# One closing stage for the RWKV branch and the gated merge, with products of split weights, in a hybrid encoder layer

## The reference, cut to what matters

```
# RWKV branch, after the two scans; 8 heads of 64 channels
y = ys[0] + ys[1]
mu = mean(y, -1); var = mean(square(y - mu), -1)
y = ((y - mu) * rsqrt(var + GN_EPS)).reshape(B, S, 512) * gn_w + gn_b
bonus = sum(r_h * k * r_k, -1) * v_h
g = sigmoid(gd) @ gate_up
y_a = ((y + bonus) * g) @ w_o_rwkv
# MLA branch: o is the attention's output
y_b = o @ w_o_mla
x = x + gate1 * ((g_a * y_a + g_b * y_b) @ w_out)
```

## Time and profile before

| | us |
|---|---|
| median of 3 runs (3070.61 to 3104.45) | 3072.3 |
| the profiled execution, its own time | 3069.41 |
| its span, first to last instruction | 3067.5 |
| PE busy in the span (86%) | 2632.4 |
| DVE busy (45%) | 1381.7 |
| ACT busy (29%) | 903.7 |
| POOL busy (24%) | 722.6 |

### The profile page before, as it was taken

The page is one execution under the profiler, slowest core; times in us unless marked ns, Lnnn a source line. Parts: engine busy times, 40 slices in busy tenths (PEclk is TensorE's granted clock), DMA queues, the critical chain, the costliest instruction groups (busy, mean ns, idle before and its releaser), DMA issues. The chain is left out here.

```text
span 3067.5 us, 55849 instructions
## 1 busy us (share of the span) xinstructions
PE 2632.4 (86%) x23155; PEld 2022.6 (66%) x23155; DVE 1381.7 (45%) x1995; ACT 903.7 (29%) x1714; POOL 722.6 (24%) x563
## 2 busy tenths in 40 slices
PE   8699999999959999996988999657968952999990
PEld 2288887788849999996974555443437742788870
DVE  2544469866623555543544556442234340111116
ACT  2311133444413555443543444340012210111110
POOL 0122245444423444430332000220000003010003
PEclk9899999999966999996988999878989866999995
DMA  8312233443341232213338110332231113999977
GB/s 349 107 69 86 86 122 138 144 141 141 119 149 43 86 86 82 86 24 123 100 89 322 32 32 1 114 106 110 109 119 55 55 43 144 354 352 355 350 291 274
DMA packets 161343, 428.64 MB, mean 140 GB/s; under 512 B 38156, under 2 KB 85172, under 8 KB 147832
## 3 DMA queue, kind: packets, MB, share of 16 engines
q1 hardware_dynamic: 131432, 322.82, 30.6%
q0 software_dynamic: 15456, 53.50, 4.5%
q10 hardware_dynamic: 14256, 49.44, 4.0%
HBM read 302.94 MB, written 122.77 MB: 139 GB/s over the span
## 5 line engine op out<-in xcount | busy, mean ns | idle before, releaser
L99 PE MATMUL ps_in<-h_t_low,w_in_high 128*128 128x512 f32 x960 | 380.3, 396 | 20.8 <-DVE h_t_low L611 20.8
L100 PE MATMUL ps_in<-h_t_high,w_in_low 128*128 128x512 f32 x960 | 375.3, 391 | 0.0
L101 PE MATMUL ps_in<-h_t_high,w_in_high 128*128 128x512 f32 x960 | 374.9, 391 | 0.0
L2510 PE MATMUL ps_hidden<-xb_turned,w_tile 128*128 128x128 f32 x2176 | 248.1, 276 | 8.2 <-ACT xb_turned L2528 8.2
L2510 PEld LDWEIGHTS ps_hidden<-xb_turned,w_tile 128*128 128x128 f32 x2176 | 245.1, 192 | 12.0 <-ACT xb_turned L2528 12.0
L99 PEld LDWEIGHTS ps_in<-h_t_low,w_in_high 128*128 128x128 f32 x960 | 181.0, 189 | 63.3 <-issue 20.7
L101 PEld LDWEIGHTS ps_in<-h_t_high,w_in_high 128*128 128x128 f32 x960 | 181.1, 189 | 38.4
L1119 POOL TENSOR_TENSOR wkv_levels<-wkv_nt,level_mask 128x1024 f32<-128x1024 f32 x60 | 140.1, 2353 | 276.6 <-ACT wkv_nt L1068 276.6
L100 PEld LDWEIGHTS ps_in<-h_t_high,w_in_low 128*128 128x128 f32 x960 | 181.1, 189 | 36.1
L1880 PE MATMUL ps_scores<-att_k,att_q 96*128 96x512 f32 x320 | 168.0, 640 | 16.2 <-DMA att_q<-qk_t 16.2
L1968 DVE TENSOR_REDUCE att_neg_max<-ps_scores 128x1 f32<-128x1024 f32 (+1 forms) x96 | 100.5, 1047 | 115.7 <-PE ps_scores L1880 115.7
(11 more groups left out here) (344 smaller groups left out, 5197.8 us busy)
## 6 DMA issues: line engine op xcount, KB each, us to landing
w_tile<-in_w SPq DMA_DIRECT2D x34, 2048.0 KB, 9.3
w_tile<-in_w SPq DMA_DIRECT2D x34, 1024.0 KB
w_ada_tile<-in_w_ada SPq DMA_DIRECT2D x12, 2048.0 KB
wkv_in<-wkv_out SPq DMA_DIRECT2D x24, 1024.0 KB, 4.7
w_in_tile<-in_w_in SPq DMA_DIRECT2D x40, 512.0 KB, 5.7
yb<-yb_tile ACTq DMA_DIRECT2D x34, 512.0 KB, 9.4
yb<-att_zeros POOLq DMA_DIRECT2D x32, 512.0 KB, 35.4
p_t<-p_mixed ACTq DMA_DIRECT2D x24, 512.0 KB
```

The lines of the kernel that those rows point to most:

```text
L99: nc.tensor.matmul(out, w[0], x[1], start=start, stop=False)
L100: nc.tensor.matmul(out, w[1], x[0], start=False, stop=False)
L101: return nc.tensor.matmul(out, w[0], x[0], start=False, stop=stop)
L2510: mm = nc.tensor.matmul(ps_h[b][:, f], w13[:, b, k, P * f:P * f + P], xt[:, b, k], start=(k == 0), stop=(k == DF - 1))
```

## The change

`finish_and_merge` takes the place of `rwkv_finish` and `merge_branches`, in one block, unrolled.

- The merge has 48 units instead of 24: first 24 for MLA (output tile by output tile, three blocks of tokens each), then 24 for RWKV (block by block, eight output tiles each). A unit is 4 products of one branch, each by `split_product`, so 12 F32R products; DVE multiplies by one gate and, in the RWKV half, adds to `merged`.
- ACT makes the high parts of `om_t` (three blocks) and of each weight tile, DVE the low parts (`om_low`, `w_low`). MLA's 8 weight tiles are split once, RWKV's 8 tiles once for each block of tokens, 32 splits in all. The closing's result is written over `om_t`, whose blocks are split again (`oa_high`, `oa_low`).
- The closing's six tiles are dealt out between the units, a new tile every PITCH = 4 units, from unit 0 on: DVE has one or two steps of it behind each unit's gate (mean, centre, variance, normalise, bonus, affine, gated_out at 0, 1, 2, 3, 4, 6 and 7 units past the tile's start), PE has the bonus sums behind unit 4j+2 and the output gate and the turning behind unit 4j+5.
- Group norm is done by token: y stays with tokens on the partitions, mean and variance are DVE reductions over 64 channels (128x16 results of 128x1024), the root is ACT's Sqrt and DVE's reciprocal of 128x16, and y is turned once, after it is normed. The matrices of ones are scaled by r_k once, so that POOL's second multiplication goes. The tanh of the output gate is one instruction for all tokens.
- SP loads y for two tiles ahead, weights in 3 buffers, gates in 4 buffers of 128x512.

```diff
-def rwkv_finish(nc, dram, consts, oa_t):
...
-def merge_branches(nc, dram, consts, oa_t, om_t, merged):
...
+def finish_and_merge(nc, dram, consts, om_t, merged):
...
+        GB, RB, PITCH = 4, 3, 4
...
+        units = [(1, df, n) for df in range(DF) for n in range(NT)] + [(0, df, n) for n in range(NT) for df in range(DF)]
...
+        first_unit = lambda w: w * NT if w < DF else half + w - DF
...
+            def load_gate(u):
+                a, df, n = units[u]
+                if u >= GB:
+                    v = u - GB
+                    if v < half:
+                        sp.wait_ge(m["gated"], v + 1)
+                    else:
+                        sp.wait_ge(m["added"], v - half + 1)
+                sp.dma_start(gate[:, u % GB], dram["gates"][a * DF + df, :, cols(n)]).then_inc(g_in[u % GB], 16)
...
+            load_w(0)
+            load_y(0)
+            sp.dma_start(head_ones[:], dram["head_ones"][:, :]).then_inc(m["ones_in"], 16)
+            load_gate(0)
+            load_rk(0)
+            load_w(1)
+            sp.dma_start(sg[:], dram["p_t"][GD]).then_inc(m["gd_in"], 16)
+            sp.dma_start(up[:], dram["gate_up"][:, :]).then_inc(m["up_in"], 16)
+            for u in range(1, GB):
+                load_gate(u)
+            load_v(0)
+            load_y(1)
+            load_w(2)
+            loaded = RB
+            for u in range(len(units)):
+                if u + GB < len(units):
+                    load_gate(u + GB)
+                while loaded < len(tiles) and first_unit(loaded - RB) - 2 <= u:
+                    load_w(loaded)
+                    loaded += 1
+                for j in range(N):
+                    if u == PITCH * j + 3 and j + 1 < N:
+                        load_rk(j + 1)
+                    if u == PITCH * j + 5 and j + 1 < N:
+                        load_v(j + 1)
+                    if u == PITCH * j + 6 and j + 2 < N:
+                        load_y(j + 2)
...
+            sum_directions(0)
+            for j in range(N):
+                pool.wait_ge(m["rk_in"], 16 * j + 16)
+                nc.gpsimd.tensor_tensor(rkv[:, 0:4], rkv[:, 0:4], rkv[:, 4:8], ALU.mult).then_inc(m["rk"], 1)
+                if j + 1 < N:
+                    sum_directions(j + 1)
...
+                pe.wait_ge(m["w_lo"], w + 1)
+                if a == 1:
+                    pe.wait_ge(m["om_lo"], n + 1)
+                else:
+                    pe.wait_ge(m["oa_lo"], n + 1)
+                if u >= 2:
+                    pe.wait_ge(m["gated"], u - 1)
+                for f in range(RF):
+                    mm = split_product(nc, ps[:, u % 2], (w_hi[:, w % 2, f], w_lo[:, w % 2, f]), (src_hi[:, f, cols(n)], src_lo[:, f, cols(n)]),
+                                       start=(f == 0), stop=(f == RF - 1))
+                mm.then_inc(m["full"], 1)
...
+            for u in range(len(units)):
+                unit(u)
+                for j in range(N):
+                    if u == PITCH * j + 2:
+                        bonus_sums(j)
+                    if u == PITCH * j + 5:
+                        output_gate(j)
+                        turn(j)
...
+            def oa_high(n):
+                act.wait_ge(m["oa"], (n + 1) * NB // PB)
+                act.wait_ge(m["full"], half - NT + n + 1)
+                nc.scalar.copy(src_hi[:, :, cols(n)], om_t[:, :, cols(n)]).then_inc(m["oa_hi"], 1)
+            def w_high(w):
+                act.wait_ge(w_in[w % RB], 16 * (w // RB) + 16)
+                if w >= 2:
+                    act.wait_ge(m["full"], first_unit(w - 1))
+                nc.scalar.copy(w_hi[:, w % 2], w_raw[:, w % RB]).then_inc(m["w_hi"], 1)
...
+            om_high(0)
+            w_high(0)
+            om_high(1)
+            om_high(2)
+            act.wait_ge(m["gd_in"], 16)
+            nc.scalar.activation(sg[:], sg[:], ACT.Tanh, scale=0.5).then_inc(m["tanh"], 1)
+            for u in range(len(units)):
+                if u + 2 in new_tile:
+                    w_high(new_tile[u + 2])
+                for j in range(N):
+                    if u == PITCH * j + 1:
+                        act.wait_ge(m["centred"], j + 1)
+                        nc.scalar.activation(sq[:], by_head(j % 2), ACT.Square).then_inc(m["squared"], 1)
+                    if u == PITCH * j + 2:
+                        act.wait_ge(m["var_in"], j + 1)
+                        nc.scalar.activation(st[:, j % 2, 2], st[:, j % 2, 1], ACT.Sqrt).then_inc(m["sqrt"], 1)
+                if u == half - NT:
+                    oa_high(0)
+                if u == half + 2:
+                    oa_high(1)
+                if u == half + 8:
+                    oa_high(2)
...
+            def gate_unit(u):
+                a, df, n = units[u]
+                dve.wait_ge(m["full"], u + 1)
+                dve.wait_ge(g_in[u % GB], 16 * (u // GB) + 16)
+                if a == 1:
+                    nc.vector.tensor_tensor(merged[:, df, cols(n)], ps[:, u % 2], gate[:, u % GB], ALU.mult).then_inc(m["gated"], 1)
+                else:
+                    nc.vector.tensor_tensor(gate[:, u % GB], ps[:, u % 2], gate[:, u % GB], ALU.mult).then_inc(m["gated"], 1)
+                    dve.wait_ge(m["gated"], u + 1)
+                    nc.vector.tensor_tensor(merged[:, df, cols(n)], merged[:, df, cols(n)], gate[:, u % GB], ALU.add).then_inc(m["added"], 1)
...
+            def centre(j):
+                dve.wait_ge(m["mean"], j + 1)
+                nc.vector.scalar_tensor_tensor(out=by_head(j % 2), in0=spread(st[:, j % 2, 0]), scalar=-1.0 / CH, in1=by_head(j % 2),
+                                               op0=ALU.mult, op1=ALU.add).then_inc(m["centred"], 1)
+            def variance(j):
+                dve.wait_ge(m["squared"], j + 1)
+                nc.vector.tensor_reduce(st[:, j % 2, 1], sq[:], AX.X, ALU.add).then_inc(m["var"], 1)
+                dve.wait_ge(m["var"], j + 1)
+                nc.vector.tensor_scalar(st[:, j % 2, 1], st[:, j % 2, 1], 1.0 / CH, GN_EPS, ALU.mult, ALU.add).then_inc(m["var_in"], 1)
+            def normalise(j):
+                dve.wait_ge(m["sqrt"], j + 1)
+                nc.vector.reciprocal(st[:, j % 2, 2], st[:, j % 2, 2]).then_inc(m["inverse"], 1)
+                dve.wait_ge(m["inverse"], j + 1)
+                nc.vector.tensor_tensor(by_head(j % 2), by_head(j % 2), spread(st[:, j % 2, 2]), ALU.mult).then_inc(m["normed"], 1)
+            def bonus(j):
+                dve.wait_ge(m["bonus_full"], j + 1)
+                dve.wait_ge(m["v_in"], 16 * j + 16)
+                if j > 0:
+                    dve.wait_ge(m["oa"], j)
+                nc.vector.tensor_tensor(z[:], ps_b[:], rkv[:, 8:12], ALU.mult).then_inc(m["bonus"], 1)
+            def affine(j):
+                dve.wait_ge(m["turned"], j + 1)
+                dve.wait_ge(m["bonus"], j + 1)
+                for f in range(RF):
+                    ins = nc.vector.scalar_tensor_tensor(out=z[:, f], in0=ps_y[:, f], scalar=col(consts, "gn_w", f, 1), in1=z[:, f], op0=ALU.mult, op1=ALU.add)
+                ins.then_inc(m["affine"], 1)
+            def gated_out(j):
+                dve.wait_ge(m["affine"], j + 1)
+                dve.wait_ge(m["gate_full"], j + 1)
+                dve.wait_ge(m["om_lo"], toks(j).start // NB + 1)
+                for f in range(RF):
+                    ins = nc.vector.scalar_tensor_tensor(out=om_t[:, f, toks(j)], in0=z[:, f], scalar=col(consts, "gn_b", f, 1), in1=ps_g[:, f],
+                                                         op0=ALU.add, op1=ALU.mult)
+                ins.then_inc(m["oa"], 1)
...
+            om_low(0)
+            w_low(0)
+            dve.wait_ge(m["ones_in"], 16)
+            for f in range(RF):
+                ins = nc.vector.tensor_scalar(head_rk[:, f], head_ones[:], col(consts, "r_k", f, 1), None, ALU.mult)
+            ins.then_inc(m["head_rk"], 1)
+            om_low(1)
+            om_low(2)
+            dve.wait_ge(m["tanh"], 1)
+            nc.vector.tensor_scalar(sg[:], sg[:], 0.5, 0.5, ALU.mult, ALU.add).then_inc(m["sig"], 1)
+            for u in range(len(units)):
+                gate_unit(u)
+                if u + 2 in new_tile:
+                    w_low(new_tile[u + 2])
+                for j in range(N):
+                    at = u - PITCH * j
+                    if at == 0:
+                        mean(j)
+                    if at == 1:
+                        centre(j)
+                    if at == 2:
+                        variance(j)
+                    if at == 3:
+                        normalise(j)
+                    if at == 4:
+                        bonus(j)
+                    if at == 6:
+                        affine(j)
+                    if at == 7:
+                        gated_out(j)
+                if u == half - NT:
+                    oa_low(0)
+                if u == half + 4:
+                    oa_low(1)
+                if u == half + 10:
+                    oa_low(2)
...
```

(50 more changed lines are left out.)

105 lines of the change are left out of this document (88 added, 17 removed).

## The result

| | before | changed |
|---|---|---|
| median, us | 3071.5 (3066.7 to 3104.5, 4 runs) | 2948.9 (2945.2 to 2951.1, 4 runs) |
| profiled execution / its span | 3069.4 / 3067.5 | 2947.8 / 2946.1 |
| both stages: their first DMA to the next stage's first | 306.7 | 180.3 |

The ratio is 0.957 (95% interval 0.952 to 0.963): faster by 4.3%. The forecast was 2953 (range 2936 to 2985).

A forecast was written before the change was run, and what follows sets the result against it. Bound: closing by a chain of waits across engines, merge by TensorE. Start 15.8, MLA 85.5 plus 9, RWKV 69.0 plus 6, end 2.4: 187.7 for 306.7 us, 119.0 off 3069.4 gives 2950.4, plus 2.9: 2953 (2936 to 2985).

The forecast's parts named there:

- Everything lies between two DMAs and counts one for one: Closing and merge, 306.7 us from their first DMA to the next stage's: what is saved there comes off the span.
- TensorE paces; products: Merge: a split product takes 0.69 us, a unit of four 2.76, 48 units 132.5 us, where 164.6 was.
- TensorE's closing work: Closing on TensorE, beside the products: bonus sums 1.8 us, gate and turning 2.8, so 4.6 a tile, 27.6 for six.
- VectorE just behind: MLA half, per tile of four units: VectorE needs 13.6 us, 14.4 with waits, against TensorE's 15.6.
- the likeliest case: The forecast itself for the whole kernel: 2953 us, chance 0.60.
- Allowances: Time added for stalls: 9 us in the MLA half (waits on GpSimd, late loads), 6 in the RWKV half.
- The start: New stage, first DMA to unit 2: 15.8 us, with gd's load at 12 us, then the tanh 1.65 and VectorE's step 1.0.
- The tightest wait: MLA half: y lands after 5.4 us, GpSimd adds 2.34, VectorE wants it 7.4 us on and waits some 3 us.
- VectorE's pace: Rival, MLA half: GpSimd instructions hold VectorE for their full length, a tile costs 19.1 us, not 15.6; 2965; chance 0.15.
- the loads' pace: Rival, MLA half: 27 MB at 237 GB/s take 114 us, for 105, with y late; 2965 to 2975; chance 0.15.
- Half clock: Rival, new stage: waits for VectorE keep TensorE at 1.2 GHz, stage 324 us, 18 more than now; 3090; chance 0.03.
- a sign: Sign that the forecast is right: MLA periods of 16 to 17.5 us for four units.

## Why the prediction was right

- *Everything lies between two DMAs and counts one for one.* Right: 126.4 us went between them, 121.4 from the span. The 5.0 between is the spread of the rest of the program (2759 to 2771 over all profiles).
- *TensorE paces; products.* Right, with 0.68 us for the product and 2.72 for the unit where I had 0.69 and 2.76; float32 products in its place cost 25.7 us. I had chosen the row of the input projection; the output projection's 0.70 would have been farther off.
- *TensorE's closing work.* 4.4 us a tile for 4.6.
- *VectorE just behind.* The 13.6 us of work a tile (14.4 with its waits) stand against 13.4 measured (73.7 us busy in the 86.6 of units 2 to 23, which are five and a half tiles), and TensorE's 15.6 against 15.3 to 16.7. So the likeliest case came out. But the margin was judged for one engine alone: with TensorE made 43 us lighter, the MLA half didn't get faster, for the loads. That TensorE leads at all is shown narrowly: the 43 us gave 8.
- *Allowances.* 9 us in the MLA half were 3.0: units 2 to 23 took 86.6, of which 83.6 are the products and the closing's work at the rates above; 2.8 of the gaps are at units 10 and 22. The 9 had been chosen between 0 and 21, not worked out, and were three times too many. Six in the RWKV half were 5.1 (unit 24 to the end of 47: 24 x 2.72 and 2.7 for gate and turning are 68.0, measured 73.1), nearly in the units named: 24 to 31 for 25 to 31, and 36 at the last block split.
- *The start.* 15.8 us were 18.0. The step that was off is the last chain ahead of the first gate: the load of gd landed after 13.1 us for 12, the tanh took 1.5, and VectorE's step behind it 2.6 for 1.0, held up by GpSimd. With both taken off that path unit 2 began after 12.6 us.
- *The tightest wait.* I named y; it was r and k, for which the prediction has no chain at all. VectorE waited for the sum of directions only 1.1 us in all, while r*k stopped TensorE twice and, with less else to do, five times. I had the 5.4 us to landing from y's loads of 0.5 MB (5.3 here); r and k, 1 MB in one load, took 7.1. The 3 us of wait for y did not come from the numbers beside them either: 5.4 and 2.34 are 7.7, for 7.4 to be had. Once r and k were ahead and TensorE lighter, y was next.
- *The rivals.* VectorE's pace and the loads' pace were each true one step behind the bound. Half clock did not hold: the granted clock went to its upper level at 1960.6, was back at the lower one from 1964.0 to 1967.4 after TensorE had stood from 1961.7 to 1964.2, and then was 1.00 to the end of the stage, in which TensorE's longest wait was 1.4 us.

The errors: start +2.2, MLA half -7.9, RWKV half -1.9, end +0.2, stage 180.3 for 187.7. The time erred by less, 2948.9 for 2953, and part of that is luck: of the 7.4 us too many in the stage, 5.0 were made up by a longer rest of the program, which leaves some 2.5 (2947.8 for 2950.4), and the median lay 1.2 above the profiled execution where I had added 2.9. The MLA periods, 15.3 us where nothing waits, also came out under the 16 to 17.5 that I had named as a sign.

## What to carry to other kernels

A chain of short steps across engines is best dealt out between the units of a stage that one engine binds; count each other engine's work per unit against that engine's, and take the uneven places one by one. When the bound is lifted, look for the resource that has one buffer and is asked for last: here a late load, not the busier engine, was next. And test small gains together too, since a gain can be hidden by the wait behind it, as the start's was by r and k.

## What the runs showed that I had not expected

GpSimd and VectorE hold each other up both ways, and a step with a single SBUF input can be caught too. At the start of the changed kernel, in the timeline:

```profile
1958.84 2.37 POOL L1985 TENSOR_TENSOR fin_y<-fin_y 128x1024 f32<-128x1024 f32 x1 [330.04 <-DMA fin_y<-wkv_y]
1958.98 2.90 DVE L2159 TENSOR_SCALAR head_rk<-head_ones,cols 128x128 f32<-128x128 f32 x4 [2.04 <-DMA head_ones<-in_head_ones]
...
1961.80 4.48 DVE L2090 TENSOR_TENSOR branch_low<-om_t,branch_high 128x2048 fp32r<-128x2048 f32 x2
1962.66 5.87 POOL L1990 TENSOR_TENSOR fin_rkv<-fin_rkv 128x1024 f32<-128x1024 f32 x1 [1.46 <-DMA fin_rkv<-p_t]
...
1966.71 2.64 DVE L2164 TENSOR_SCALAR fin_gate<-fin_gate 128x1536 f32<-128x1536 f32 x1 [0.42 <-ACT fin_gate L2068]
```

Of the four scalings of 128x128, each 0.28 us when free, the first took 2.3 and ended with GpSimd's sum; then GpSimd's product, 2.4 us when free, took 5.9: it began during the first of two block splits and ended 2.2 us after the second; and the output gate's step took 2.6, of which 1.8 passed before that product ended (0.94 in the run with the earlier first gate, where GpSimd stood idle). The Trainium skill, page "SBUF — State Buffer", section "Who interferes with whom", says that a tensor_scalar can enter a mode that takes the port pair shared with GpSimd, that whoever issues first has this pair for the whole instruction, and that the other blocks. The trace agrees. I had counted two-input steps only, and so missed 1.6 us of the 2.2 by which the start was off.
